# Attention heads of the mixer handled in pairs on TensorE, in a two-layer hybrid encoder step on one NeuronCore

## The reference, cut to what matters

```python
def diff_core(q, k, v, lam, mask):          # group C
    s = jnp.einsum('bqhcd,bkhcd->bhcqk', q, k) * (D_C ** -0.5)
    p = softmax(where(mask, s, -inf), axis=-1)
    a = p[:, :, 0] - lam * p[:, :, 1]
    return jnp.einsum('bhqk,bkhe->bqhe', a, v)

def gla_chunk(s0, q, k, v, lg):             # group A, chunks of 64 tokens
    att = einsum('bthd,bshd,btshd->bhts', q, k, decay)
    o = att @ v + (q * exp(b)) @ s0
    s1 = exp(b_last) * s0 + (k * exp(b_last - b)).T @ v
```

## Time and profile before

| what | value |
| --- | --- |
| runs before, median of 3 | 1540.67 us (1539.06 to 1540.74) |
| profiled execution, its own time | 1540.56 us |
| its span | 1538.8 us |
| mean granted clock of TensorE | 0.997 of full speed |
| PE busy | 1527.8 us (99%) |
| DVE, ACT, POOL busy | 1235.8 us, 998.2 us, 218.8 us |
| loop over the heads, layer 0 | from 67.9 us to 134.8 us of the span |
| loop over the heads, layer 1 | from 455.9 us to 523.5 us |

### The profile page before, as it was taken

The page is one execution under the profiler, slowest core; times in us unless marked ns, Lnnn a source line. Parts: engine busy times, 40 slices in busy tenths (PEclk is TensorE's granted clock), DMA queues, the critical chain, the costliest instruction groups (busy, mean ns, idle before and its releaser), DMA issues.

```text
span 1538.8 us, 21554 instructions
## 1 busy us (share of the span) xinstructions
PE 1527.8 (99%) x8400; PEld 1329.6 (86%) x8400; DVE 1235.8 (80%) x1255; ACT 998.2 (65%) x1079; POOL 218.8 (14%) x249
## 2 busy tenths in 40 slices
PE   9999999999999999999999999999999999999998
PEld 7989999999998978888888888888888888888886
DVE  5877666654577758988889898998988988998897
ACT  5565533333455547777777778777777777777774
POOL 5514400001150413101001001002002002002000
PEclk9999999999999999999999999999999999999999
DMA  8333455444433459999999999999999999999994
GB/s 226 96 110 118 148 162 165 139 149 151 130 117 109 142 211 335 398 372 387 373 375 382 380 370 370 396 363 378 384 367 379 380 361 377 395 367 366 399 363 179
DMA packets 159701, 437.43 MB, mean 284 GB/s; under 512 B 12068, under 2 KB 66176, under 8 KB 145264
## 3 DMA queue, kind: packets, MB, share of 16 engines
q1 hardware_dynamic: 151796, 423.02, 74.8%
q0 software_dynamic: 5552, 9.62, 2.4%
q10 hardware_dynamic: 2252, 3.41, 0.8%
HBM read 429.40 MB, written 13.60 MB: 288 GB/s over the span
## 4 chain that ended last, share of the span: by engine, by line
PE 97%; DVE 1%; ACT 1%; DMA 0%; issue 0%; SPq 0%; DVEq 0%; ACTq 0%
PE bank L1975 33%; PE bank L2473 13%; PE bank L2484 13%; PE bank L2477 13%; PE bank L2495 7%; PE bank L2498 7%; PE bank L2504 7%; PE bank L1978 3%; PE bank L2513 2%; DMA gla<-b_g 0%; DVE x L1966 0%; DVE cut_lo L1339 0%; ACT cut_hi L908 0%; DVE gla L1487 0%; DVE xgT_lo L1960 0%
## 5 line engine op out<-in xcount | busy, mean ns | idle before, releaser
L1801 DVE TENSOR_TENSOR split_lo<-raw,split_hi 128x2048 fp32r<-128x2048 f32 x336 | 762.8, 2289 | 99.8 <-ACT split_hi L1202 98.8
L1202 ACT CAST split_hi<-raw 128x2048 fp32r<-128x2048 f32 x336 | 640.4, 1911 | 223.1 <-PE bank L2484 144.3
L2473 PE MATMUL bank<-split_hi,xgT_hi 128*128 128x512 f32 x896 | 291.5, 395 | 0.2 <-ACT xgT_hi L1249 0.2
L2477 PE MATMUL bank<-split_hi,xgT_lo 128*128 128x512 f32 x892 | 285.8, 390 | 0.0
L2484 PE MATMUL bank<-split_lo,xgT_hi 128*128 128x512 f32 x896 | 240.0, 390 | 0.0
L908 ACT CAST cut_hi<-ring 128x1024 fp32r<-128x1024 f32 x124 | 129.9, 1048 | 166.6 <-PE bank L1975 166.2
L1975 PE MATMUL bank<-xT_hi,cut_hi 128*128 128x320 f32 x752 | 236.5, 314 | 0.5 <-DVE cut_lo L1339 0.5
L1975 PE MATMUL bank<-xT_hi,cut_lo 128*128 128x320 f32 x752 | 233.1, 310 | 0.0
L1975 PE MATMUL bank<-xT_lo,cut_hi 128*128 128x320 f32 x752 | 231.6, 308 | 0.0
L1339 DVE TENSOR_TENSOR cut_lo<-ring,cut_hi 128x1024 fp32r<-128x1024 f32 x124 | 153.0, 1234 | 80.7 <-ACT cut_hi L908 80.1
L2484 PEld LDWEIGHTS bank<-split_lo,xgT_hi 128*128 128x128 f32 x896 | 168.2, 188 | 34.9
(11 more groups left out here) (306 smaller groups left out, 1599.1 us busy)
## 6 DMA issues: line engine op xcount, KB each, us to landing
raw<-moe_w_gate SPq DMA_DIRECT2D x112, 1024.0 KB, 8.5
raw<-moe_w_up SPq DMA_DIRECT2D x112, 1024.0 KB, 8.0
raw<-moe_w_down SPq DMA_DIRECT2D x112, 1024.0 KB, 7.4
ring<-w_in SPq DMA_DIRECT2D x15, 1024.0 KB, 5.5
ring<-ffn_w_gate SPq DMA_DIRECT2D x11, 1024.0 KB, 5.5
ring<-ffn_w_up SPq DMA_DIRECT2D x11, 1024.0 KB, 5.3
ring<-ffn_w_down SPq DMA_DIRECT2D x10, 1024.0 KB, 5.0
ring<-w_out SPq DMA_DIRECT2D x8, 1024.0 KB, 5.0
```

Source lines behind the costliest of these rows:

```text
L1202: return nc.scalar.copy(split_hi[:, i % SR, :], raw_piece(i)).then_inc(hi_ready, 1)
L1801: V.tensor_tensor(split_lo[:, i % SR, :], raw_piece(i), split_hi[:, i % SR, :].bitcast(F32), ALU.subtract).then_inc(lo_ready, 1)
L2473: TE.matmul(o, xgT_hi[:, kk, :], hi[:, w * k + 512 * c:w * k + 512 * c + 512], start=kk == 0, stop=False)
L2477: TE.matmul(o, xgT_lo[:, kk, :], hi[:, w * k + 512 * c:w * k + 512 * c + 512], start=False, stop=False)
```

## The change

Scores of two heads, (1,2), (3,4), (5,6), (7,8) and (9,10), are made in one go in the odd turn, the odd head in the right half of banks 4 and 5 and the even one in the left half; heads 0 and 11 stay alone. Odd turns then also make the value products of heads n - 5 and n - 4 and the transposes of heads n - 3 and n - 2. Even turns hold none of the three. The across halves keep their turn numbers; in odd turns they stand ahead of the value products, and in even turns behind F(n), ahead of what fills the turn. DVE waits, ahead of `most` of an even head, until the head before has left the banks. Sums of squares and their sources move by up to a turn.

```diff
-    for _n in range(HEADS + 2):
-        if _n == HEADS:
-            JOBS["T"].append(("hist", _l))
-        if _n >= 2:
-            JOBS["T"].append(("at", _l, _n - 2))
+    for _n in range(HEADS):
+        if _n % 2 and _n >= 3:
+            JOBS["T"] += [("at", _l, _n - 3), ("at", _l, _n - 2)]
...
-    JOBS["T"].append(("ya", _l, 2))
+    JOBS["T"] += [("hist", _l), ("at", _l, HEADS - 2), ("at", _l, HEADS - 1), ("ya", _l, 2)]
...
-        scores_of = score_banks[:, :, 0:256]
+        scores_of = [score_banks[:, :, 256 * (n % 2):256 * (n % 2) + 256] for n in range(HEADS)]
...
-                    if n >= 2:
+                    if n % 2 and n >= 3:
+                        probs_T(n - 3)
                         probs_T(n - 2)
-                    if n in (6, 10):
-                        squares_oc((n - 6) // 4)
+                    if n in (7, 11):
+                        squares_oc((n - 7) // 4)
                     probs(n)
...
                     dve.wait_ge(RS.full, RS.filled(("s", l, n)))
+                    if n and n % 2 == 0:
+                        dve.wait_ge(RS.free, RS.emptied(("s", l, n - 1)))
...
-                    if n == 7:
+                    if n == 8:
                         sum_squares(l, "oc", 0, TILES[0][1], H)
-                    if n == 8:
                         sum_squares(l, "oa", 2, TILES[2][1], H)
...
                         state(2)
-                        sum_squares(l, "oc", 1, TILES[1][1], H)
...
                 lo(q0 + N_IN)
+                sum_squares(l, "oc", 1, TILES[1][1], H)
...
+                def pair_scores(first, count):
+
+                    for n in range(first, first + count):
                         pe.wait_ge(RT.free, RT.emptied(("qt", l, n // H)))
-                    pe.wait_ge(RS.free, RS.n["s", l, n])
-                    scores(n, 0)
-                    scores(n, 1).then_inc(RS.full, 1)
+                    pe.wait_ge(RS.free, RS.n["s", l, first])
+                    for n in range(first, first + count):
+                        scores(n, 0)
+                        last = scores(n, 1)
+                    last.then_inc(RS.full, count)
+
+                def crossing(n):
+
                     if n in (4, 5):
                         inner(n - 4, True)
                     if n in (6, 7):
                         update(n - 6, 2 * (n - 6) + 1)
                     if n in (8, 9, 10):
                         recurrent((n - 6) % 3, True)
-                    if n >= 2:
-                        differ_T(n - 2)
-                    if n >= 3:
-                        attended(n - 3)
+
+                for n in range(HEADS):
+                    if n == 0:
+                        pair_scores(0, 1)
+                    if n % 2:
+                        pair_scores(n, 2 if n < HEADS - 1 else 1)
+                        crossing(n)
+                        if n >= 5:
+                            attended(n - 5)
+                            attended(n - 4)
+                        if n >= 3:
+                            differ_T(n - 3)
+                            differ_T(n - 2)
                     features(RC, (FILL[n][0], l, FILL[n][1]))
+                    if n % 2 == 0:
+                        crossing(n)
...
                 ya_T(RS, 1)
+                attended(HEADS - 4)
+                attended(HEADS - 3)
                 differ_T(HEADS - 2)
-                attended(HEADS - 3)
```

More of the change, by code:

```diff
@@ L1020, in probs @@
                         act.wait_ge(am_ready, HEADS * l + n - 1)
-                    s = scores_of
+                    s = scores_of[n]
                     for c in range(2):
@@ L1623, in most @@
                     dve.wait_ge(RS.full, RS.filled(("s", l, n)))
-                    V.tensor_reduce(nm[0:rows, n % 2], scores_of[0:rows, :, 0:keys], AX_X, ALU.max,
+                    if n and n % 2 == 0:
+                        dve.wait_ge(RS.free, RS.emptied(("s", l, n - 1)))
+                    V.tensor_reduce(nm[0:rows, n % 2], scores_of[n][0:rows, :, 0:keys], AX_X, ALU.max,
                                     negate=True).then_inc(nm_ready, 1)
@@ L2136, in scores @@
                     t0, rows = TILES[t]
-                    b = scores_of
+                    b = scores_of[n]
                     q0 = HW * c
@@ L2241, in differ_T @@
                     last.then_inc(RT.full, 1)
-                for n in range(HEADS):
-                    if n % H == 0:
+                def pair_scores(first, count):
+                    for n in range(first, first + count):
                         pe.wait_ge(RT.free, RT.emptied(("qt", l, n // H)))
-                    pe.wait_ge(RS.free, RS.n["s", l, n])
-                    scores(n, 0)
-                    scores(n, 1).then_inc(RS.full, 1)
+                    pe.wait_ge(RS.free, RS.n["s", l, first])
[4 more added lines that the diff above has]
+                def crossing(n):
                     if n in (4, 5):
```

## The result

The changed kernel takes 1561.31 us (median of 4, 1560.52 to 1563.23) against 1539.87 us before on the same chip (1538.49 to 1540.74): a ratio of 1.0139, 95% interval 1.0127 to 1.0151. It is 21 us slower, more than twice the 9.7 us that were forecast, and outside the range.

The account below looks back on a forecast made before the run. TensorE, holding 97% of the chain, was taken to bound the kernel: 1540.56 + 10.4 for uncovered hand-overs - 0.8 for fewer changes of kind = 1550.2 us, 1550.3 against the median. The range was 1546 to 1555.5 us.

Parts of the forecast that it names:

- Part 3, the stalls: Even turns 4 to 10: across halves behind F leave ring D's hand-overs uncovered, 5.2 us a layer, 10.4 us in both.
- The clock falls in the holes: Rival, chance 0.07: idling in turn 6 makes F(7) run at 1.2 GHz, 3.6 us more a layer, 1557.5 us.
- Part 1, fewer changes of kind: PE's transposes no longer followed by value products in the loop: net 0.4 us a layer saved, 0.8 us in all.
- Part 2, overlap of scores: Scores of two heads in a row on PE: nothing booked; upper bound about 0.4 us a pair, 4 us over both layers.
- Small items: Around F(2), `vc` waits go and `lo` is late next: net nothing, bounds -1.3 and +0.3; DVE's new wait costs nothing.
- rivals of absorption: Rival, chance 0.04: the expert stage gives layer 1's part of the loss back, 1545.5 us.
- no change: Rival, chance 0.03: stalls half as long, 2.6 us a layer, and the scores' overlap, about 1540.6 us.

Follow-up runs that it names:

- third experiment: The changed kernel with useless matmuls filling PE's holes in turns 6 and 10: 1552.66 us, ratio 1.0078 to the kernel before.
- first experiment: The changed kernel with the across halves of even turns ahead of F(n) again, pairs kept: 1541.50 us, ratio 1.0008 to the kernel before.
- experiment 4: The changed kernel, DVE taking head 6's maximum before `state(0)`, ACT making head 10's exponentials before `squares_oa(1)`: 1550.30 us, ratio 1.0061 to the kernel before.
- experiment 8: The changed kernel with turn 6's across half ahead of F(6) again, plus 12 useless matmuls ahead of F(10): 1555.03 us, ratio 1.0086 to the kernel before.

## Why the prediction was wrong

- *Part 3, the stalls: right.* Every wait came at the place and with the engine named, within 0.1 us: turn 4 0.37 (0.3), turn 6 1.16 and 1.32 (1.2 and 1.3), turn 8 0.94 (1.0), turn 10 0.96 and 0.34 (1.0 and 0.4), in both layers. By starts they cost 5.7 us a layer; I had 5.2. The missing half microsecond is the 0.07 to 0.16 us ahead of each that the brackets don't count.
- *The step that failed: the clock was left out of the sum.* "The clock falls in the holes" was a rival of 0.07, "short" holes speaking against it, and priced for turn 6 alone at 3.6 us a layer, 1557.5 us. It happened behind turn 6 and behind turn 10 of both layers, and cost 9.1 us: 3.0 us for each hole in layer 0 and 1.5 to 1.6 us in layer 1. So the rival had the price of a hole too high and their number too low. By the books the forecast was short by 10.9 us: 9.1 for the clock, 1.0 for the stalls (11.4 instead of 10.4) and 0.8 for part 1. The rows I had could not show it: the only stretch under full clock there was the start. That should have made it an open term with an upper bound of one section and its F block for each hole, in the range, not a rival with a low chance. The warning of the Trainium skill, TensorE: Matmul & The Clock Gate, Why this matters for your kernels, against idle gaps amid matmul bursts, is borne out in kind by the third experiment: with the holes filled the clock goes from 0.50 back to 1.00. The gaps that the page names are longer than the waits of 1.16 and 1.32 us here; the measurement decides.
- *Part 1, fewer changes of kind, -0.8 us: not seen.* The first experiment has all of it and is no faster. In its turn 5 two products and two transposes take 0.66 us (94.99 to 95.65); in the kernel before one of each takes 0.31 us (89.47 to 89.78 in turn 4, 95.38 to 95.69 in turn 5), 0.62 us for two. Putting like with like saved nothing there.
- *Part 2, overlap of scores: taken as 0, measured 0.2 us a pair,* half of the upper bound. It shows at 128 keys too, which my reading of the single heads had spoken against: the pair (1,2) costs 0.65 us in the change (73.03 to 73.68) where two singles cost 0.86. By the Trainium skill, TensorE: Matmul & The Clock Gate, Part 3 (Packing small matmuls), small matmuls in different row groups run at nearly the price of one; the 0.65 us go that way, and by far not all of it. Which matmuls overlap in a pair is not shown.
- *Small items: right.* The waits on `vc` went, `cut_lo` came in their place (1.2 us in layer 1, 0.3 in layer 0). In layer 0 F(2) began 10.33 us behind turn 0's scores, before 10.58 us, the 0.25 us that I had given; in layer 1 nothing moved. DVE's new wait cost nothing visible. The tail of layer 0 began 11.1 us behind and ended 11.87 us behind. It is 0.8 us longer in the first experiment too, where nothing waits, so this is work that moved into it from the loop and no delay. Nothing was given back up to the start of layer 1's loop, 11.89 us behind.
- *The rivals of absorption and of no change* fall with experiment 1: what the holes cost arrives whole at the end.

## What to carry to other kernels

Before a producer's second half is moved across a long block of work, ask who empties its buffer and what covered that: a ring with one bank is only as good as the block between hand-over and next job. And price a hole on TensorE twice, as its length and as what may stand behind it at half clock, here 1.5 to 3 us a hole. The remedy is to put the cover back, which won 20 us of 21 (first experiment). Where a hole can't be avoided, useless matmuls into a bank that is overwritten anyway can fill it; here they won back 9 us of 21.

## What I had not expected of the hardware

One hole of 1.2 us (experiment 4), or waits of 0.96 and 0.34 us with 0.5 us of work between them (experiment 8), in a stream that is otherwise full, can bring the granted clock from 1.00 to 0.50. Half clock then lasted 3 to 6.5 us, though PE was busy all the time. The same hole passed unpunished in the other layer of one execution (experiment 8) and, by the mean clocks, in other executions (experiment 4). Turn 8's hole of 0.94 us brought no fall in any of the profiles. What such a hole costs differs from one execution to the next, and comparisons of such versions need several.
